# A Fourier mixer turned into a real transform of half the columns, with folded weights and a mirrored residual

## What is computed

```python
def fourier_mix(h, w_f):
    b, n, d = h.shape
    hg = h.astype(jnp.float32).reshape(b, n, N_FOURIER_GROUPS, FOURIER_GROUP)
    f = jnp.fft.fft2(hg, axes=(1, 3), norm="ortho").real
    return f.reshape(b, n, d).astype(h.dtype) @ w_f
...
    hx = modulate(rms_norm(x, norm_g[i, 1]), mx[3], mx[4])
    x = x + mx[5] * fourier_mix(hx, fourier_w[f])
```

## Time and profile before

| | |
|---|---|
| time of the runs | 3094.22 us median (3092.47, 3094.22, 3095.91) |
| span of the profiled execution | 3089.3 us (its whole time is not recorded apart; the median is 4.9 us above the span) |
| TensorE busy | 2972.2 us, 96% |
| the stage's matmuls, first to last | 1793.45 to 1903.98 us: 110.5 us |
| mean granted TensorE clock | 0.986 |

### The profile page before, as it was taken

How to read it: one execution, slowest core, us unless ns; L and a number is a source line. 1 busy time by engine, 2 the same in 40 slices (tenths; PEclk the granted TensorE clock), 3 DMA queues, 4 the chain that set the end, 5 groups by cost and what they waited for, 6 DMA issues and landing times.

```text
span 3089.3 us, 38183 instructions
## 1 busy us (share of the span) xinstructions
PE 2972.2 (96%) x15170; PEld 2308.7 (75%) x15170; DVE 1374.2 (44%) x2200; ACT 902.4 (29%) x1423; POOL 267.3 (9%) x310
## 2 busy tenths in 40 slices
PE   8999999999989999999999999999999988999995
PEld 7888888877846788888888888888888765774442
DVE  5636343445587564654333334333342357531113
ACT  4112121232175322223222233222233356221111
POOL 1000000001100100001000011000010146012221
PEclk9999999999999999999999999999999999999998
DMA  7232323221000355543232212222232300448995
GB/s 284 99 117 102 132 97 128 79 81 55 28 1 28 143 224 184 206 180 105 94 102 95 83 40 82 95 95 97 84 122 95 116 28 1 151 157 347 364 363 237
DMA packets 78206, 395.80 MB, mean 128 GB/s; under 512 B 17536, under 2 KB 19968, under 8 KB 51328
## 3 DMA queue, kind: packets, MB, share of 16 engines
q1 hardware_dynamic: 66560, 385.65, 34.0%
q0 software_dynamic: 11520, 8.43, 0.9%
HBM read 444.34 MB, written 16.78 MB: 149 GB/s over the span
## 4 chain that ended last, share of the span: by engine, by line
PE 87%; DVE 7%; ACT 2%; DMA 2%; issue 2%; POOL 1%; SPq 0%; DVEq 0%; ACTq 0%; POOLq 0%
PE ps L860 16%; PE ps L861 16%; PE ps L862 16%; PE ps L3037 5%; PE ps L3059 3%; PE ps L2070 2%; PE ps L2071 2%; PE ps L2072 2%; PE ps L1547 2%; PE ps L1225 1%; PE ps L1566 1%; PE ps L1813 1%; PE ps L1226 1%; PE ps L1815 1%; PE ps L1227 1%
## 5 line engine op out<-in xcount | busy, mean ns | idle before, releaser
L860 PE MATMUL ps<-h_high_ffn,weights_high_ffn 128*128 128x512 f32 (+1 forms) x1696 | 623.9, 368 | 2.9 <-DVE weights_low_ffn L1004 2.9
L861 PE MATMUL ps<-h_low_ffn,weights_high_ffn 128*128 128x512 f32 (+1 forms) x1696 | 623.6, 368 | 0.0
L862 PE MATMUL ps<-h_high_ffn,weights_low_ffn 128*128 128x512 f32 (+1 forms) x1696 | 623.2, 367 | 0.0
L860 PEld LDWEIGHTS ps<-h_high_ffn,weights_high_ffn 128*128 128x128 f32 x1696 | 320.4, 189 | 57.2 <-issue 3.9
L862 PEld LDWEIGHTS ps<-h_high_ffn,weights_low_ffn 128*128 128x128 f32 x1696 | 320.0, 189 | 53.0
L861 PEld LDWEIGHTS ps<-h_low_ffn,weights_high_ffn 128*128 128x128 f32 x1696 | 320.3, 189 | 52.4
L950 ACT ACTIVATE weights_high_ffn<-weights 128x2048 fp32r<-128x2048 f32 (+4 forms) x160 | 243.7, 1523 | 341.3 <-PE ps L862 276.4
L860 PE MATMUL ps<-hidden_high_ffn,weights_high_ffn 128*128 128x512 f32 (+1 forms) x880 | 327.2, 372 | 14.0 <-issue 6.9
L1004 DVE TENSOR_TENSOR weights_low_ffn<-weights,weights_high_ffn 128x2048 fp32r<-128x2048 f32 (+4 forms) x160 | 289.5, 1809 | 82.6 <-ACT weights_high_ffn L950 81.0
L861 PE MATMUL ps<-hidden_low_ffn,weights_high_ffn 128*128 128x512 f32 (+1 forms) x880 | 325.6, 370 | 0.0
L862 PE MATMUL ps<-hidden_high_ffn,weights_low_ffn 128*128 128x512 f32 (+1 forms) x880 | 325.2, 370 | 0.0
(11 more groups left out here) (459 smaller groups left out, 4465.4 us busy)
## 6 DMA issues: line engine op xcount, KB each, us to landing
weights<-in_ffn_gu SPq DMA_DIRECT2D x88, 1024.0 KB, 4.9
big<-in_w_exp_gu SPq DMA_DIRECT2D x32, 2048.0 KB, 9.5
scratch_ffn<-in_w_mod SPq DMA_DIRECT2D x35, 1536.0 KB, 6.5
weights<-in_ffn_d SPq DMA_DIRECT2D x24, 768.0 KB, 4.2
weights<-in_w_in SPq DMA_DIRECT2D x16, 1024.0 KB, 4.8
weights<-in_ffn_d SPq DMA_DIRECT2D x24, 640.0 KB, 3.9
weights<-in_w_exp_dn SPq DMA_DIRECT2D x15, 1024.0 KB
hbuf<-in_w_exp_dn SPq DMA_DIRECT2D x12, 1024.0 KB
```

Of the source, the lines that this page charges most:

```text
L860: pe.matmul(out, wh, xh, start=(k == 0), stop=False)
L861: pe.matmul(out, wh, xl, start=False, stop=False)
L862: mm = pe.matmul(out, wl, xh, start=False, stop=(k == n - 1))
```

## The change

- The feature table has 256 columns in place of 512: 129 cosines (0 to 128) and 127 sines (1 to 127). The cosine of column 0 is halved in the table.
- A has 8 units; each takes two token blocks into the two halves of one bank (12 matmuls of 256 columns).
- The token tables have 258 columns (tokens 0 to 257) in place of 512. B gives 9 results: for each group one of cosines ("even") and one of sines ("odd"), each of 12 matmuls of 258 columns, and one of 97 rows that holds cosine 128 of the four groups (on partitions 0, 32, 64 and 96), whose weights are read from `Y` with a step of 8 elements.
- The output weights are folded: GpSimd adds the rows of f and of 256-f for the even part and subtracts them for the odd part (`fold_weights`), two instructions of 128 x 1024 for each slab. The row of f = 128 is a table of its own (`nyquist`).
- C makes an odd product (12 matmuls) and an even one (12, and 3 with the row of f = 128) in two banks for each output tile, for tokens 0 to 257. ScalarE scales the odd one by the gate into tokens 0 to 256, and by the negative gate, read backwards, into tokens 257 to 511 (`odd_part`); VectorE adds that to `xy` (`add_odd`), then the even one, forwards and backwards (`residual`).
- The scaled input (`full`) is held in two PSUM banks and no longer in SBUF, so `scale_in(k)` waits for `input_low(k-2)`.
- The ring buffers are given back by GpSimd after a fold, no longer by TensorE after the low part.
- ScalarE no longer counts up `room_act` in the feed-forward and in the next mixer (nobody waited for it); VectorE makes `neg_gate` once (128 x 8).

```diff
-        C = 2 * (D // groups)
-        units = groups * TT
+        C = D // groups
+        HALF = NX // 2
+        NF = HALF + 2
+        units, spectra = groups * TT // 2, 2 * groups + 1
+        MIRROR = 2 * groups
+        NYQ = 3 * 32 + 1
...
+                for v in range(units):
+                    g = v // 2
+                    if v % 2 == 0:
                         pe.wait_ge(in_low.sem, j0 + 2 * g + 2)
+                    if v >= 5:
+                        pe.wait_ge(low.sem, b0 + v - 4)
+                    for i in range(2):
+                        t = v % 2 * 2 + i
+                        tok = slice(t * P, (t + 1) * P)
+                        for k in range(2):
+                            mm = three(unit(v)[:, i * C:(i + 1) * C], h_high[:, 2 * g + k, tok], h_low[:, 2 * g + k, tok],
+                                       cd_high[:, k, :], cd_low[:, k, :], k == 0, k == 1)
                     mm.then_inc(product.sem, 1)
+                for i in range(MIRROR):
+                    g, c = i // 2, i % 2
+                    pe.wait_ge(low.sem, b0 + max(2 * (g + 1), units + i - 4))
+                    transform(i, c, lambda Y, t: Y[:, t, g, c * P:(c + 1) * P])
+                pe.wait_ge(low.sem, b0 + units + MIRROR - 4)
+                transform(MIRROR, 0, lambda Y, t: Y[:, t].rearrange("p g c -> p (g c)")[:, P:P + 8 * NYQ:8])
...
+                    if m % 2 == 0:
+                        pe.wait_ge(fm["wo_low"].sem, k0 + slab_order(n))
+                    if m >= 3:
+                        pe.wait_ge(fm["wo_added"].sem, r0 + m - 2)
+                    if m == 0:
+                        pe.wait_ge(low.sem, b0 + units + MIRROR)
...
+                def fold_weights(n):
+                    s = n % 2
+                    gpsimd.wait_ge(ring.landed[s], 16 * (n0[s] + n // 2 + 1))
+                    left, right = ring.buf[:, s, 0:SLOT // 2], ring.buf[:, s, SLOT // 2:SLOT]
+                    gpsimd.tensor_tensor(folded[n][:, 0:SLOT // 2], left, right, ALU.add)\
+                        .then_inc(folded_weights.sem, 1)
+                    gpsimd.tensor_tensor(folded[n][:, SLOT // 2:SLOT], left, right, ALU.subtract)\
+                        .then_inc(folded_weights.sem, 1)
+                    gpsimd.wait_ge(folded_weights.sem, 2 * n + 2)
+                    gpsimd.sem_inc(ring.used[s], 1)
...
+                fold_weights(1)
+                gpsimd.wait_ge(product.sem, p0 + units)
+                fold_weights(2)
+                fold_weights(3)
...
+                def add_odd(m):
+                    vector.wait_ge(high.sem, a0 + units + spectra + m + 1)
+                    step(vector.tensor_tensor(xy[:, m, 0:NX], xy[:, m, 0:NX], odd[m % 2], ALU.add))
+
                 def residual(m):
...
+                    vector.scalar_tensor_tensor(xy[:, m, 0:HALF + 1], even_bank(m)[:, 0:HALF + 1], gate[:, m, 0:1],
+                                                xy[:, m, 0:HALF + 1], ALU.mult, ALU.add)
+                    vector.scalar_tensor_tensor(xy[:, m, HALF + 1:NX], even_bank(m)[:, HALF - 1:0:-1], gate[:, m, 0:1],
+                                                xy[:, m, HALF + 1:NX], ALU.mult, ALU.add).then_inc(fm["wo_added"].sem, 1)
```

More of the change, by code:

```diff
@@ L136, in build @@
     warm = sb("warm", [P, 1])
+    neg_gate = sb("neg_gate", [P, KD])
     inverse = sb("inverse", [P, 2, KT])
@@ L410, in gains_of_mods @@
                                              normg[:, j * KD:(j + 1) * KD, 0:n], ALU.add, ALU.mult))
+        if i == 1:
+            step(vector.tensor_scalar(neg_gate[:], mods[1][:, 5 * KD:6 * KD, 0], -1.0, None, ALU.mult))
         halve(vector, i, gates)
@@ L961, in item @@
                         scalar.wait_ge(act_done[s].sem, t * ns + (a0[s] + (turn0 + 1) * ns))
-                        scalar.sem_inc(room_act.sem, 1)
                         scalar.activation(a_high[:, ds(t * 2 + s, 1), :].rearrange("p a n -> p (a n)"),
@@ new lines, in fourier_mixer @@
+        HALF = NX // 2
[3 more added lines that the diff above has]
+        NYQ = 3 * 32 + 1
+        Y_high, Y_low = (placed(f"fourier_{p}", at * K1, [P, TT, groups, C], F32R) for p, at in (("high", 0), ("low", 16)))
+        h_high, h_low = (placed(f"fourier_h_{p}", at * K1, [P, KD, NX], F32R) for p, at in (("high", 48), ("low", 64)))
+        F_high, F_low = (placed(f"fourier_out_{p}", at * K1, [P, spectra, NF], F32R) for p, at in (("high", 48), ("low", 58)))
@@ new lines, in fourier_mixer @@
+        cd_high, cd_low = (placed(f"dft_feature_{p}", at * K1, [P, 2, C], F32R) for p, at in (("high", 80), ("low", 82)))
+        cn = placed("dft_token", 93 * K1, [P, 2 * TT, NF])
+        cn_high, cn_low = (placed(f"dft_token_{p}", at * K1, [P, 2 * TT, NF], F32R) for p, at in (("high", 84), ("low", 93)))
+        folded = [placed(f"fourier_w_folded{n}", at * K1, [P, SLOT]) for n, at in enumerate((102, 118, 68, 32))]
+        w_low = [placed(f"fourier_w_low{n}", at * K1, [P, SLOT], F32R) for n, at in enumerate((102, 118, 68, 32))]
@@ L1792, in fourier_mixer @@
+        odd = [placed(f"fourier_odd{b}", (84 + 2 * b) * K1, [P, NX]) for b in range(2)]
         names = (scaled, in_high, in_low, nm["early_high"], nm["early_low"], proj_done[0], raw_done[0], raw_done[1],
@@ L1992, in fourier_mixer @@
         tables.at += 32
-        for c, n in zip(names, (KD, KD, KD, 5, 5, units + KD, units + KD, units + KD, 4, 4, KD, KD)):
+        loaded.at += 16
+        done = units + spectra
+        for c, n in zip(names, (KD, KD, KD, 5, 5, done, done + KD, done, 5, 5, 2 * KD, KD)):
             c.at += n
@@ L3278, in layouts @@
     L["w_o"] = slabs(a["attn_w_o"][0], 2)
-    L["w_f"] = slabs(a["fourier_w"][0], 2)
+    mix = a["fourier_w"][0].reshape(4, D // 4, D)
+    halves = (mix[:, 0:P], mix[:, (-np.arange(P)) % (D // 4)])
+    L["w_f"] = np.concatenate([slabs(w.reshape(4 * P, D), 2) for w in halves], axis=2)
+    L["w_f_nyquist"] = np.zeros((P, D), np.float32)
+    L["w_f_nyquist"][::32] = mix[:, P]
     W = D // 4
```

237 lines of the change are left out of this document (131 added, 106 removed).

## The result

| | before | after |
|---|---|---|
| time of the runs | 3094.74 us median (3092.47 to 3095.91, 4 runs) | 3046.49 us median (3045.22 to 3048.42, 4 runs) |
| ratio after / before | | 0.9846, interval 0.9832 to 0.9860 |
| span of the profiled execution | 3089.3 us | 3045.4 us |
| mean granted TensorE clock | 0.986 | 0.982 |

What follows compares the result with a forecast made beforehand. TensorE's 480 matmuls of 512 columns bound the stage. 58.6 us gained, less 0.12 at the start, 1.85 for the port and 0.2 at the end, gave 56.5: 3094.2 - 56.5 = 3037.7 us, range 3034 to 3047.

Steps and rivals of the forecast that it cites:

- The price of the stream: TensorE in A, B and C: 0.1195 us a matmul of 256 columns, 0.1204 of 258, together 50.5 us.
- plain fp32 rate: Rival in B and C: 258 columns run at 0.456 us a matmul, 148 us, whole 3147 us; chance 0.02.
- loads that set the pitch: Rival on TensorE: weight loads of 0.188 us set the pitch, 28.5 us more, whole 3066 us; chance 0.03.
- VectorE bounding C: Rival in C: backward reads over 1.6 us make VectorE the bound; at 2 us, whole 3042 us; chance 0.04.
- The slow stretch at A's start: TensorE at A's start: 3.0 us at the lower clock stay after the wait for input tiles, costing 1.4 us.
- The port: Late in B: VectorE and GpSimd exclude each other on SBUF operands, so TensorE idles 1.85 us at result 8.
- slab 0's low part runs 1809.06 to 1811.34: Step of the engine clock in B: VectorE's low part goes between the two halves of GpSimd's fold 2.
- the first rival: In B: GpSimd keeps the port through folds 2 and 3, TensorE idles 7 us, whole 3044 us; chance 0.17.
- The half clock behind it: Within the port rival: the 1.85 us of idleness bring a stretch of slow TensorE clock, whole 3039 us.
- The stepped loads: In B: twelve 97-column weight loads with a step of 8 elements cost nothing, at worst 2.3 us.
- Backward reads: In C: 255 columns read backwards from PSUM cost as forwards, 0.4 us, at worst 0.75.
- the end: Behind C: the last residual and sum of squares take longer, mostly hidden by fillers; 0.2 us lost.

Runs made afterwards that it cites:

- fold2_behind_low0: Changed kernel with GpSimd starting slab 2's folds only once VectorE has made slab 0's low part; one run of 3043.16 us.
- before_again: The kernel before the change, run once more without edit for a second profile; 3092.99 us, ratio 0.9999.
- splits_gather: Changed kernel with VectorE's f = 128 and slab 1 low parts behind B's nine, and ScalarE copying the 97 stepped columns together; 3040.27 us, ratio 0.9818.

## Why the prediction was right and wrong

**The price of the stream: right.** Starts are 0.12 us apart in all three steps, for 256 and for 258 columns; C without half clock takes 25.68 us from the first to the last of 216, 0.1194 each. The rivals of plain fp32 rate, of loads that set the pitch and of VectorE bounding C are out. The Trainium skill's rule (TensorE: Matmul & The Clock Gate, The mechanism, in Part 3) does not hold here: each of these matmuls loads its own 128 rows, and 91 us were not needed.

**The slow stretch at A's start: wrongly kept.** The term of 1.4 us did not come in 13 of 15 profiles, with 1.95 us of idleness, while the kernel before had its slow stretch in 3 of 3 behind 1.85 us; A is 12.14 us, not 12.9, and that includes a wait of 0.3 us that I had not seen.

**The port: the mechanism was right, the size was not.** The term was 1.85 us of idleness; it measured 2.69, with 0.4 us more at results 5 and 7. The step that failed is "slab 0's low part runs 1809.06 to 1811.34", ahead of fold 2's second half. My clock had the fold's first half end at 1809.06 and slab 0's high part at 1809.02: a dead heat, which I gave to VectorE by the argument that it asks while the first half runs, though by these times it hardly did. In the chip the second half was issued 0.01 to 0.03 us earlier in all 13 profiles with this order of work, so slab 0's low part waited a half fold too, and the turns went against VectorE once more. fold2_behind_low0, where my order holds, has 1.6 us of wait. The Trainium skill (SBUF — State Buffer, Who interferes with whom) has the pair of ports as an exclusive lock whose holder is the one that issues first: the 0.03 us, with 4.52 us in place of 2.29 behind them, agree. That a queued fold lets a VectorE instruction in between which already waits, as I assumed, held each time; so the first rival, with TensorE idle for 7 us at result 4, did not come.

**The half clock behind it: in the wrong place of the sum.** I had it in a rival ("the 1.85 us of my own clock bring a slow stretch, 3039"), not in the forecast, since 1.61 us had brought none. It cost 1.5 us here.

**The stepped loads: the term of 0 was mis-sized.** Taken as nothing with a bound of 2.3 us, they cost 0.8: 12 x 0.065.

**Backward reads, the end, C:** right. 255 columns backwards take VectorE 0.47 us as 257 forwards take 0.48, C has no wait, and the distance from the last matmul to the sums is 2.20 us in place of 2.24, so that even the 0.2 us at the end did not come.

Together in the stage: 53.4 us saved for 56.5 forecast (56.8 us from A's first matmul to C's last, where I had written about 54). A gave 0.8 back; B took 2.9 more than forecast (the wait with its restart 1.0, small waits and restarts 1.1, step and half clock 0.8) and C's half clock 1.2; the 0.2 at the end did not come.

**The rest, some 5 us, was no term at all,** and it is the largest step that failed: of the 8.3 us between 56.5 and 48.2, 3.1 are in the stage and 5.2 outside it. I moved the gain of a stage one to one to the whole; the profiles show the first layer's feed-forward, the router and the experts 1.9, 1.3 and 3.0 us longer in its place, for causes that are open in part. The profiled execution before was also a quick one: its span was 3.4 us below that of before_again (3092.7), so "the runs' median lies 4.9 above the span" held an accident of 3 us. For one execution the whole time and the span lie only 1.8 us apart (3040.27 and 3038.5 in splits_gather).

## What to carry to other kernels

Where GpSimd works from SBUF beside VectorE's SBUF to SBUF instructions, count each such pair as turns of whole instructions, for both engines, and ask which result stands in the queue behind them: moving two instructions behind nine short ones was worth 4.5 us in the stage, with slab 0's low part still at 4.52 us. Forecast a wait together with what may follow it, a stretch at half clock, and leave the size of both as a range when your own clock has two issues within a tenth of a microsecond. And look at a change's stage and at the whole apart: the stage repeats to 0.2 us, while single executions of the whole changed kernel went from 3037.36 to 3051.20 and its medians of 4 or 5 from 3044.95 to 3046.49.

## What the hardware showed that I had not expected

- With instructions waiting on both sides VectorE and GpSimd took turns by whole instructions in every profile here, and GpSimd is held up as much as VectorE: folds of 2.4 us took 4.23 and 3.36 us. VectorE's reads of PSUM (258 columns) beside them kept 0.41 us.
- A weight load of 97 columns with a step of 8 elements (32 bytes) raises the distance of two starts from 0.12 to 0.185 us. ScalarE copies the same 388 elements a partition in 0.98 us.
- Half clock behind a wait is neither certain nor tied to its length: at A's start 1.85 us brought it in 3 of 3 profiles of the kernel before and 1.95 us in 2 of 15 of the changed one, and the 2.7 us in B in 7 of 8. Behind those, it began 0.3 to 2.0 us after the work had started again. Filling the wait in B left none both times.
